# Block sums of a weight stream, made by DMA in DRAM, issued at other places of a two-layer transformer kernel, with five short VectorE steps placed elsewhere

## Reference

```python
def first_block(x, ...):            # DEPTH = 1, mixer 0
    h = rmsnorm(x, norm_g[0, 0])
    h = fox_attention(h, fox_w_in, fox_b_f, fox_w_out)   # 16 heads of 128, softmax with a forget bias
    x = x + rmsnorm(h, norm_g[0, 1])
    h = sqrelu_mlp(rmsnorm(x, norm_g[0, 2]), mlp_w1, mlp_w2)   # 2048 -> 8192 -> 2048
    return x + rmsnorm(h, norm_g[0, 3])

def hybrid_layer(x, ...):           # second block
    h = rms_norm(x, norm_g)
    q, k, v, z_a, u_b, v_b, z_b, g_a, g_b = split(h @ w_in)
    att = moba_attention(norm(q), norm(k), v)            # 8 heads of 128, here one causal block of 256
    y_a = (att * silu(z_a)) @ w_proj_a
    y_b = (spatial_gating(gelu(u_b), gelu(v_b)) * silu(z_b)) @ w_proj_b
    return x + (sigmoid(g_a) * y_a + sigmoid(g_b) * y_b) @ w_out
```

## Time and profile before

| | us |
|---|---|
| median of 3 executions (lowest, highest) | 1756.34 (1756.19, 1756.82) |
| the profiled execution's own time | 1755.75 |
| its span | 1753.9 |
| PE busy, share of the span | 1744.2, 99% |
| DVE busy | 1428.1, 81% |
| ACT busy | 957.4, 55% |
| POOL busy | 240.5, 14% |
| SP's stream queue, share of the 16 DMA engines | 56.9% |
| POOL's queue, share of the 16 DMA engines | 15.9% |
| sums: copies (512 KB) and adds (256 KB) | 65 and 65 |

### The profile page before, as it was taken

The page is one execution under the profiler, slowest core; times in us unless marked ns, Lnnn a source line. Parts: engine busy times, 40 slices in busy tenths (PEclk is TensorE's granted clock), DMA queues, the critical chain, the costliest instruction groups (busy, mean ns, idle before and its releaser), DMA issues.

```text
span 1753.9 us, 23934 instructions
## 1 busy us (share of the span) xinstructions
PE 1744.2 (99%) x8698; PEld 1479.5 (84%) x8698; DVE 1428.1 (81%) x1864; ACT 957.4 (55%) x1306; POOL 240.5 (14%) x324
## 2 busy tenths in 40 slices
PE   9999999999999999999999999999999999999999
PEld 8888888878888888888888887888888888888887
DVE  6557777886799779878987887999888899995798
ACT  7434444556555445644654555767655566554454
POOL 1023434111000200110011000002222100000000
PEclk9999999999999999999999999999999999999999
DMA  9787777886867986797688776687576656666566
GB/s 330 250 272 219 226 234 215 258 277 185 248 210 235 259 261 213 235 271 246 213 231 272 239 227 229 192 232 244 196 207 209 202 175 217 214 206 201 178 197 191
DMA packets 111296, 399.70 MB, mean 228 GB/s; under 512 B 13632, under 2 KB 14288, under 8 KB 109776
## 3 DMA queue, kind: packets, MB, share of 16 engines
q1 hardware_dynamic: 93536, 333.23, 56.9%
q0 software_dynamic: 16800, 64.78, 15.9%
q10 hardware_dynamic: 864, 0.44, 0.1%
HBM read 387.89 MB, written 53.23 MB: 252 GB/s over the span
## 4 chain that ended last, share of the span: by engine, by line
PE 91%; DVE 6%; ACT 1%; issue 1%; DMA 1%; POOL 0%; DVEq 0%; ACTq 0%; POOLq 0%
PE bank L541 22%; PE bank L562 16%; PE bank L826 12%; PE bank L546 12%; PE bank L827 12%; PE bank L828 12%; DVE w_lo L1773 2%; PE bank L578 1%; PE bank L612 1%; DMA raw<-in_stream 1%; PE bank L691 1%; ACT w_hi L1189 1%; PE bank L749 1%; PE bank L734 1%; PE bank L740 0%
## 5 line engine op out<-in xcount | busy, mean ns | idle before, releaser
L1773 DVE TENSOR_TENSOR w_lo<-raw,w_hi 128x1024 fp32r<-128x1024 f32 x620 | 748.2, 1224 | 208.7 <-ACT w_hi L1189 205.5
L1189 ACT ACTIVATE w_hi<-raw 128x1024 fp32r<-128x1024 f32 x620 | 647.5, 1055 | 438.2 <-PE bank L546 153.1
L541 PE MATMUL bank<-h_both,w_hi 128*128 128x512 f32 x1792 | 434.7, 395 | 0.0
L541 PEld LDWEIGHTS bank<-h_both,w_hi 128*128 128x128 f32 x1792 | 330.8, 188 | 66.0
L546 PEld LDWEIGHTS bank<-h_both,w_lo 128*128 128x128 f32 x1792 | 229.8, 191 | 8.7
L546 PE MATMUL bank<-h_both,w_lo 128*128 128x256 f32 x1792 | 232.5, 283 | 0.0
L826 PE MATMUL bank<-w_hi,h_both 128*128 128x512 f32 (+1 forms) x382 | 148.4, 389 | 0.6 <-DVE w_lo L1773 0.6
L828 PE MATMUL bank<-w_lo,h_both 128*128 128x512 f32 (+1 forms) x382 | 147.8, 387 | 0.0
L827 PE MATMUL bank<-w_hi,h_both 128*128 128x512 f32 (+1 forms) x382 | 147.8, 387 | 0.0
L562 PE MATMUL bank<-w_hi,a_both 128*128 128x512 f32 x448 | 138.9, 391 | 0.0
L826 PE MATMUL bank<-w_hi,a_both 128*128 128x512 f32 x320 | 124.7, 390 | 1.8 <-DVE w_lo L1773 1.8
(11 more groups left out here) (342 smaller groups left out, 2509.1 us busy)
## 6 DMA issues: line engine op xcount, KB each, us to landing
raw<-in_stream SPq DMA_DIRECT2D x557, 512.0 KB, 4.4
summed<-in_stream POOLq DMA_DIRECT2D x65, 512.0 KB, 7.6
raw<-summed SPq DMA_DIRECT2D x65, 512.0 KB, 4.4
summed<-in_stream POOLq DMA_DIRECT2D x65, 256.0 KB, 6.9
wide<-scaled POOLq DMA_DIRECT2D x21, 256.0 KB, 5.1
res<-in_x SPq DMA_DIRECT2D x4, 512.0 KB, 7.5
rowg<-in_norm_rows POOLq DMA_DIRECT2D x2, 1024.0 KB, 10.2
gate<-cum_rows POOLq DMA_DIRECT2D x1, 2048.0 KB, 8.1
```

The source lines that it names most:

```text
L541: pe.matmul(tile_sum[b][:, :], w_hi[:, slot + half, k * P:(k + 1) * P], h_both[:, 8 * half + k, :], start=half == 0 and k == 0, stop=False)
L1189: nc.scalar.activation(w_hi[:, slot, :], raw[:, slot, :], ACT.Copy).then_inc(hi_ready, 1)
L1773: nc.vector.tensor_tensor(w_lo[:, slot, :], raw[:, slot, :], w_hi[:, slot, :].bitcast(F32), ALU.subtract).then_inc(lo_ready, 1)
```

## The change

The sums are renumbered, since the first four are no longer made in `fox_v`. Sums 0 to 15 are made in the 16 fox heads; 16 to 19 early in `mlp`; 20 to 40 in the tile stages of mlp groups 1 to 3; 41 to 44 in the last 16 chunks of `mlp`, after POOL's load of `rowg` and ahead of `pow_post(2)`; 45 to 56 in the moba heads, one in each even head and two in each odd one; 57 and 58 in the first group of `gates`; 59 to 64 in `proj_b` and `proj_a`. None is left in `fox_v`, `fox_out` and `qkv`. The number stays 65.

In `boundary` the total of the second token half's squares is taken ahead of `norm_block(norm, 1)`. In the first moba head `soften` stands ahead of `next_rest(c + 4)` and `normalise` ahead of `next_rest(c + 5)`. The four late `sgu_lo` are made one by one behind the four steps of the second group of `gates`, where all four stood behind step 2 of the first.

```diff
@@ DVE, boundary
                 next_rest(e + 5)
+                total(1)
                 norm_block(norm, 1)
-                total(1)
                 next_rest(e + 6)
@@ DVE, moba head h
+                if h == 0:
+                    soften(n, mask)
                 next_rest(c + 4)
-                soften(n, mask)
+                if h:
+                    soften(n, mask)
                 scale_tile(b, c + 4, tile + 2)
+                if h == 0:
+                    normalise(n)
                 next_rest(c + 5)
-                normalise(n)
+                if h:
+                    normalise(n)
@@ DVE, gates group i, behind step q
-                    if i == 0 and q == 2:
-                        for k, g in enumerate(LATE_SGU):
-                            sgu_lo(g, sgu_late[:, k, :], MOBA_HEADS - len(LATE_SGU) + k + 1)
+                    if i == 1:
+                        sgu_lo(LATE_SGU[q], sgu_late[:, q, :], MOBA_HEADS - len(LATE_SGU) + q + 1)
@@ POOL, fox_v
             copy_chunk(0)
-            sum_chunks(0, FIRST["fox_v"], (20, 23, 26, 29))
@@ POOL, fox heads, fox_out
                 stage_fox(h, h == 0)
-                sum_chunk(4 + h)
-            sum_chunks(20, FIRST["fox_out"], range(2, 26, 3))
+                sum_chunk(h)
@@ POOL, mlp
-            sum_chunks(28, FIRST["mlp"], range(14, 26, 3))
+            sum_chunks(16, FIRST["mlp"], range(14, 26, 3))
...
-                    sum_chunks(32 + 7 * (w // 2 - 1), WIDE_FIRST[MLP_FIRST + w] - 32, range(2, 30, 4))
+                    sum_chunks(20 + 7 * (w // 2 - 1), WIDE_FIRST[MLP_FIRST + w] - 32, range(2, 30, 4))
...
             pool.dma_start(rowg[:, :], norm_rows[1:2, :].broadcast_to([P, D])).then_inc(rowg_in, 16)
-
+            sum_chunks(41, FIRST["mlp"] + 240, (1, 4, 7, 10))
 
             pow_post(2)
@@ POOL, qkv
-            sum_chunks(32 + 7 * (FF_GROUPS - 1), FIRST["qkv"], range(18, 50, 8))
             pool.wait_ge(sgu_in, 32)
@@ POOL, moba head h
+                if h % 2:
+                    sum_chunk(45 + h + h // 2)
                 if h + 1 < MOBA_HEADS:
                     pool.wait_ge(qk_turned, h + 1)
                     scale_qk(h + 1)
-                sum_chunk(36 + 7 * (FF_GROUPS - 1) + h)
+                sum_chunk(45 + h + (h + 1) // 2)
+
+            sum_chunks(57, WIDE_FIRST[GATES_FIRST], (4, 12))
+            sum_chunks(59, FIRST["proj_b"], range(2, 26, 4))
```

## The result

| | kernel before | changed kernel |
|---|---|---|
| median of 20 executions (lowest, highest), us | 1756.4 (1754.92, 1758.9) | 1759.7 (1757.78, 1761.88) |
| the profiled execution, us (span) | 1755.75 (1753.9) | 1758.99 (1757.2) |

The ratio of the runs is 1.002, with a 95% interval of 1.0013 to 1.0026: the change makes the kernel 3.3 us (0.2%) **slower**, where the forecast was 3.5 us faster. Of the changed kernel's page the row of engines shows why averages don't help here: PE is busy for 1744.6 us, as before.

The account below looks back on a forecast made before the run. PE was taken as the bound, busy 1744.2 of 1753.9 us, so gains lie only in its idle places. Terms summed to -3.2, with about 0.3 from smaller waits -3.5: 1756.34 to 1752.8 us, range 1751.0 to 1755.6.

Parts of the forecast that it names:

- Sums out of fox_out: Wide group of fox_out: PE's stall at 357 should go, -1.41 us (bounds 0.79 and 1.41); the one at 340 stays.
- (3): Rival: fox_out bound by DVE, 357 stall shrinks by 0.79 only, mask's block shows elsewhere; -2.4, 1753.9 us; chance 0.08.
- (5): Rival: in fox_out the change doesn't move the load that matters; without the 1.41, -2.1, 1754.2 us; chance 0.06.
- Sums out of qkv: Third wide group of qkv: POOL's mask comes earlier, PE's stall at 1203 goes, -0.51 us; otherwise 0 to +0.4.
- First moba head: End of first moba head, 1280: probabilities ready 1.67 us sooner, -1.45 us (bounds -0.8 and -1.53).
- Totals: Both boundaries: DVE's wait for POOL's root shrinks by at most 0.20 each; -0.3 us together (bounds -0.4 and 0).
- Late low parts: First gates group, 1442: DVE is 1.3 us earlier without four products; -0.35 us (bounds -0.44 and +0.3).
- Sums in moba heads: Moba heads, up to two sums each: DMA engines' share below that of the full fox heads, so 0.
- Sum 58 in gates: Second gates group: its pair beside that group's first loads may cost 0.1 us, counted within the -0.35.
- Sums into the end of mlp: Second boundary: chained copies behind rowg delay POOL's root; +0.8 us, PE itself losing 0.5 (bounds 0 and 9.8).
- The sign that the prediction had set for this: Second boundary: forecast wrong if POOL's root starts more than 2 us after DVE's L1970.
- The slower rival (4): Second boundary: above 1759.9 us if toll passes 7.8, from about 11.1 us a copy; chance 0.04.

Follow-up runs that it names:

- e10: Kernel of e8 with sums 16 to 19 moved from early mlp into the middle of fox_out; 1755.33 us, ratio 0.9995.
- e7: Kernel of e1 with POOL's mask taken ahead of the four sums of qkv; 1753.35 us, ratio 0.9982.
- e1: Kernel before with the three VectorE edits alone, all sums at their old places; 1753.67 us, ratio 0.9982.
- e8: Changed kernel with sums 41 to 44 in qkv behind the mask, odd heads' sum behind the scaling, sum 58 after 36 gates chunks; 1751.42 us, ratio 0.9974.
- e4: Changed kernel with the first sum of each odd moba head issued behind the scaling of q and k; 1757.39 us, ratio 1.0005.
- e5: Changed kernel with sum 58 issued after 36 chunks of gates instead of 12; 1757.95 us, ratio 1.0009.
- e2: Changed kernel with DVE's order as before, so only the sums are spread anew; 1760.77 us, ratio 1.0027.
- e6: Changed kernel with the four late sgu_lo back behind step 2 of the first gates group; 1759.39 us, ratio 1.002.
- e9: Changed kernel with sum 44 issued behind both roots of the second boundary, leaving three sums ahead of them; 1758.22 us, ratio 1.0011.
- e3: Changed kernel with sums 41 to 44 moved from the end of mlp to qkv, every four chunks; 1758.64 us, ratio 1.0016.

## Why the prediction was wrong

**Sums out of fox_out (-1.41): right, a little small.** -1.96 in the profile, of which 1.42 at 357; e10 shows that it is the sums: PE stalls at 354 and 360 with them, none with the same code without them. Rivals (3) and (5) are out. The stall hung on both of DVE's waits that the working names, not on the last alone: in e7 the load of the second landed in 4.13 us and that wait is gone, the one before it is there (1.12), and PE still waits 0.89.

**Sums out of qkv (-0.51): right.** -0.63 in the changed profile and in e7, where on POOL the mask alone was moved. DVE is held at the mask's new place too, but briefly: one DVE product of 128x128 takes 1.06 us instead of 0.29 at 1118, and PE feels nothing of it.

**First moba head (-1.45): right** (-1.56 in the changed kernel and in e1). **Totals (-0.3): right in kind;** 0.29 in each boundary of e1, so twice the sum's figure and past its bound of 0.4 for both. **Late low parts (-0.35):** -0.57 and nothing back, in e1, past the bound of 0.44. Had the change been these alone, the forecast for it (-2.1) would have stood beside a measured -2.6.

**Sums in moba heads priced at 0: the first failed step.** The prediction looked at the DMA engines' share, which was not what decided: at 1299 the engines are at 1.08 in the changed kernel, which stalls, and at 1.00 in e8, where PE is full. It did not follow POOL's own queue, though the diff puts the odd heads' first sum ahead of `scale_qk`: 1.1 us of issuing pushes four POOL products onto a DVE instruction that they hold. Of the three odd heads that have a scaling, heads 1 and 5 lost 1.4 and 1.2 us; in head 3 DVE was held as long as in head 5 (1.78) and PE lost 0.1. Against the kernel before, e4 stands at +1.2 by medians and the changed kernel at +3.3, so 2.1 came back; in e4's profile heads 1 to 7 lose nothing. The prediction had the mechanism at hand, for the mask at 1201, and used it only where the change removed it.

**Sum 58 in gates priced at 0.1: the second.** The prediction's own row (8.22 us to land for a load beside a sum) applied to the loads at 1443.9 to 1446.1, and these feed a group of seven products where DVE has little in hand (busy 4.91 of 5 us in e5, with PE full). Measured 2.12 in the profile and nothing of it in e5's; by medians e5 stands at +1.9 for +3.3.

**Sums into the end of mlp (+0.8): mis-sized; the third.** The mechanism was right: POOL stood in the waits for the copies and PE in the wait for the residual. The place lost 2.16, and the term that was too short is the chain of copies. At first sight it looks exact: copy 44 landed at 1079.7 where 1079.9 was worked out, and PE turned the block at 1083.01 where the working had 1082.9. That agreement is luck. The working started from `rowg`'s issue at 1051.11 in the kernel before; the changed kernel was 1.8 us ahead by then and issued it at 1049.29. From that issue to the landing of copy 44 it took 30.4 us where 28.8 had been worked out. `rowg` landed after 8.6 us, not 11.1, and copy 42 4.5 behind it, not 2.5. Copies 43 and 44 took 6.86 and 8.35, together the two medians of 7.6. **What the sum left out is POOL's own time in each link:** the add goes out 0.5 us after a landing and the next copy 0.54 behind the add, so each link is 1.04 longer than its copy, 2.1 for the two. From the landing to PE's turn it took 3.3 and not 3.0. In all the chain was 1.9 us longer than forecast, and PE, which came 1.7 us earlier than before, waited 2.19 where the working had 0.5.

The sign that the prediction had set for this fired: POOL's root (1081.88) starts 4.1 us after DVE's L1970 (done at 1077.79), more than 2. From 1070 to 1100 the profiles with all four sums lost 2.1 us (e2), 2.3 (changed, e5), 3.5 (e4) and 4.7 (e6), a late weight chunk at 1075 in all but the changed kernel included; in e4 and e6 copy 44 took 9.1 and 9.9. The fall of the clock (below) is not what made the toll.

The slower rival (4) named this chain, at copies of 11 us or more, as the only way to lose. It took no slow copies: copies 43 and 44 averaged the 7.6 of the forecast. The boundary's 2.2 alone would not have outweighed gains of 5.0; the two losses elsewhere did, which had been priced at nothing or 0.1 (2.7 in the heads, 2.1 at the start of the second group of gates).

## What to carry to other kernels

When steps are moved on a queue, read what now stands behind each of them on that queue, at every place, before reading how full the DMA engines are; a step that costs its own engine 1.1 us can push the next onto an instruction of another engine. When a chain of DMAs each waits for the one before, add the issuing engine's own time to every link, and start the chain and the engine that will wait for it from the same, changed, times: two errors can otherwise cancel in the one and not in the other. When a change moves many things at once, the parts may differ in sign: here the three VectorE edits were worth -2.6 us, the sums' new places +4.5 (which do not quite add up to the whole +3.3), and with three of those places mended the whole -4.6.

## What the runs showed of the hardware

**PE's clock after a wait.** In the changed kernel PE stood for 2.19 us, to 1083.01. From 1084 the granted clock is down to 0.50, the lower of the two levels (1.2 GHz), until about 1087.5:

```profile
1083.00:1084.00 1.00, 0.99 (x6) 0.82 (x7) 1.00 (x2) 0.52 (x2) 0.00 (x0) 1.00 0.74 74
1084.00:1085.00 1.00, 1.00 (x5) 0.85 (x4) 0.87 (x4) 0.58 (x3) 0.00 (x0) 0.55 1.12 336
1085.00:1086.00 1.00, 1.00 (x3) 0.77 (x3) 0.85 (x2) 0.71 (x3) 0.00 (x0) 0.50 0.68 209
...
1087.00:1088.00 1.00, 1.00 (x7) 0.96 (x6) 1.00 (x3) 0.54 (x3) 0.92 (x3) 0.75 0.30 45
1088.00:1089.00 1.00, 1.00 (x6) 0.81 (x5) 1.00 (x4) 0.72 (x3) 0.89 (x2) 1.00 0.86 291
```

Two matmuls take 1.05 us there in place of 0.62. From the first turn of the residual block the next 16 matmuls take 4.52 us, where e5 and e9 need 2.98 and 2.96: 1.5 us lost. But PE was then no longer ahead of what feeds it, and it has it nearly all back by 1100: from the same turn to the same matmul there it took 17.65 us, against 17.60 in e5 and 17.58 in e9, which stayed at 1.00. The same fall came in e4 (after 3.03 us) and e6 (2.89), and it cost under 0.2 net there too. No fall came after waits of 1.98 us in e9 and 1.82 in the changed kernel, both at the start of the second group of gates, nor after 1.41 in e5 and 1.43 in e9.

**POOL can hold DVE for a whole train of products, and does not always.** POOL's four products are 0.36 us apart. In head 5, DVE's product of two SBUF tensors, caught behind the first, did not come through between them but ended 0.3 us after the last, at 1369.96 against 1369.67. POOL's train took no more than in e4 (1.69 against 1.65). In head 1, DVE's product starts 0.3 us ahead of the train in five of the six profiles with the sum first; in three (changed, e5, e6) it took 2.24 to 2.25 and ended behind the train, in two (e3, e9) it came through in 1.28 and 1.30, and POOL's train took 2.17 instead. PE's loss before `turn_probs` follows it: 1.3 to 1.4 us in the first three, 0.6 in the other two. What decides between the two outcomes is open.
